# A decoder layer's merge: the first step's eight gate projections placed between the chunks of the second mixer

## The reference, cut to what matters

```python
u = rms_norm(h, mix_norm)
z = u @ w_in + b_in
aq, ak, av, bq, bk, bv, ga, gb = jnp.split(z, np.cumsum(SPLITS)[:-1].tolist(), axis=-1)
ya = dilated_attention(heads(aq), heads(ak), heads(av), rel_bias)
yb = sliding_window_sink_attention(heads(bq), heads(bk), heads(bv), sinks, rel_bias)
merged = jax.nn.sigmoid(ga) * (ya @ w_branch_a) + jax.nn.sigmoid(gb) * (yb @ w_branch_b)
h = h + merged @ w_out
```

## Time and profile before

| | before |
|---|---|
| median of 3 runs | 2120.92 us (2117.65 to 2121.31) |
| profiled execution | 2117.81 us, of it 2116.0 us span |
| PE busy | 2046.4 us, 97% of the span |
| DVE, ACT, POOL busy | 1401.3, 795.7, 177.8 us |
| mean granted clock of PE | 0.986 |

### The profile page before, as it was taken

The page is one execution under the profiler, slowest core; times in us unless marked ns, Lnnn a source line. Parts: engine busy times, 40 slices in busy tenths (PEclk is TensorE's granted clock), DMA queues, the critical chain, the costliest instruction groups (busy, mean ns, idle before and its releaser), DMA issues.

```text
span 2116.0 us, 26479 instructions
## 1 busy us (share of the span) xinstructions
PE 2046.4 (97%) x9404; PEld 1659.8 (78%) x9404; DVE 1401.3 (66%) x2333; ACT 795.7 (38%) x1485; POOL 177.8 (8%) x152
## 2 busy tenths in 40 slices
PE   7999999999999999999879999998999999999996
PEld 5878888888888777777658888887878888888885
DVE  4976667666987454566883444447877666666976
ACT  6343333334454333534452212124342333334453
POOL 4000000000032000241520000003000000000012
PEclk9999999999999999999889999999999999999998
DMA  4232233266444111000002111113222333267433
GB/s 174 80 104 97 103 110 110 75 225 244 138 151 168 40 41 40 31 31 31 21 11 110 50 60 50 50 69 126 75 101 99 105 110 110 75 222 244 139 103 110
DMA packets 82076, 213.21 MB, mean 101 GB/s; under 512 B 8923, under 2 KB 8959, under 8 KB 80032
## 3 DMA queue, kind: packets, MB, share of 16 engines
q1 hardware_dynamic: 69568, 164.66, 22.8%
q10 hardware_dynamic: 11392, 44.06, 5.8%
q0 software_dynamic: 992, 2.88, 0.4%
HBM read 158.58 MB, written 52.98 MB: 100 GB/s over the span
## 4 chain that ended last, share of the span: by engine, by line
PE 88%; DVE 8%; issue 2%; ACT 1%; DMA 0%; POOL 0%; DVEq 0%; SPq 0%; ACTq 0%; POOLq 0%
PE bank L1830 19%; PE bank L1831 19%; PE bank L1832 19%; PE bank L1786 9%; PE bank L1788 8%; PE bank L1787 8%; PE bank L1981 1%; PE bank L2018 1%; PE bank L1994 1%; DVE sp L1669 1%; DVE sp L1625 1%; DVE B_l L1239 1%; DVE wl L1204 1%; DVE op_l L1274 0%; PE bank L2050 0%
## 5 line engine op out<-in xcount | busy, mean ns | idle before, releaser
L1830 PE MATMUL bank<-B_h,op_h 128*128 128x512 f32 x624 | 250.0, 401 | 18.7 <-DVE op_l L1274 13.3
L1786 PE MATMUL bank<-xh,wh 128*128 128x512 f32 x640 | 256.0, 400 | 0.0
L1788 PE MATMUL bank<-xh,wl 128*128 128x512 f32 x640 | 250.0, 391 | 0.0
L1787 PE MATMUL bank<-xl,wh 128*128 128x512 f32 x640 | 249.9, 391 | 0.0
L1830 PE MATMUL bank<-T_h,op_h 128*128 128x512 f32 x640 | 249.1, 389 | 0.2 <-DVE U L1365 0.2
L1832 PE MATMUL bank<-T_h,op_l 128*128 128x512 f32 x640 | 249.0, 389 | 0.0
L1831 PE MATMUL bank<-T_l,op_h 128*128 128x512 f32 x640 | 249.0, 389 | 0.0
L1831 PE MATMUL bank<-B_l,op_h 128*128 128x512 f32 x624 | 246.9, 396 | 0.0
L1832 PE MATMUL bank<-B_h,op_l 128*128 128x512 f32 x624 | 246.5, 395 | 0.0
L1830 PE MATMUL bank<-gs_h,op_h 128*128 128x512 f32 x616 | 240.5, 390 | 0.7 <-DVE gs_l L1308 0.7
L1832 PE MATMUL bank<-gs_h,op_l 128*128 128x512 f32 x616 | 239.7, 389 | 0.0
(11 more groups left out here) (191 smaller groups left out, 3503.5 us busy)
## 6 DMA issues: line engine op xcount, KB each, us to landing
gr<-g_ops SPq DMA_DIRECT2D x154, 256.0 KB, 2.7
raw<-stream SPq DMA_DIRECT2D x56, 512.0 KB, 3.5
gate<-ffn_in SPq DMA_DIRECT2D x44, 512.0 KB, 4.0
up<-ffn_in SPq DMA_DIRECT2D x44, 512.0 KB, 4.9
g_ops<-tT SPq DMA_DIRECT2D x78, 256.0 KB, 2.0
g_ops<-gb SPq DMA_DIRECT2D x58, 256.0 KB, 5.1
A<-ffn_down ACTq DMA_DIRECT2D x6, 1536.0 KB, 8.1
h_spill<-h ACTq DMA_DIRECT2D x32, 256.0 KB, 2.2
```

What stands on the lines that cost most here:

```text
L1786: nc.tensor.matmul(out, wh[slot][:, cols], hi, start=first, stop=False)
L1787: nc.tensor.matmul(out, wh[slot][:, cols], lo, start=False, stop=False)
L1788: return nc.tensor.matmul(out, wl[slot][:, cols], hi, start=False, stop=last)
L1830: nc.tensor.matmul(out, op_h[slot][:, cols], hi, start=first, stop=False, skip_group_check=True)
```

## The change

The four gate tiles of merge step 0 (two tiles of output, two gates each; eight jobs) become jobs of the plan. The list of tiles is now ..., q7, g0, q8, g1, q9, g2, g3, and a job stands in every chunk from 24 to 35, one in chunk 38 and one after chunk 39. For a gate's job DVE writes its product with `rstd` to `stage` (one buffer for each half) instead of `scaled`, and ACT, in place of the bias, issues a DMA of 256 KB to a new HBM buffer `gz`. After its mixing work, POOL issues the loads back to `z_in`, two of 256 KB for each t: t = 0 at once, t = 1 once the transposes of chunk 38 are done (it loads over `sp2`), t = 2 after the last `pv` and the sum of t = 0 (it loads over that t's buffer), t = 3 after the sum of t = 1. Merge step 0 then makes only the 6 and 12 matmuls for each t; ACT takes the sigmoid in place in `z_in` with the gate's bias, and DVE multiplies `z_in` by the bank. The weight units keep their number (56); those of the first step now pass through the plan's slots.

```diff
@@ proj_tiles @@
-    return out + [("q", u) for u in range(A_UNITS + 1, HEAD_UNITS)]
+    for u in range(A_UNITS + 1, HEAD_UNITS):
+        out += [("q", u), ("g", u - A_UNITS - 1)]
+    return out + [("g", GATES - 1)]
@@ attention_plan @@
-            n_jobs = (1, 2, 1, 2)[s] if u < A_UNITS else (0, 1, 0, 1)[s] if u < HEAD_UNITS - 1 else 0
+            n_jobs = (1, 2, 1, 2)[s] if u < A_UNITS else 1 if u < HEAD_UNITS - 1 else (0, 0, 1, 0)[s] if u < HEAD_UNITS else (1, 0, 0, 0)[s]
@@ buffers @@
+    stage = [place(f"stage{s}", [P, HALF], at(20 + 2 * s)) for s in range(2)]
+    z_in = [[place(f"z_in{t}{g}", [P, HALF], at(k)) for g, k in enumerate(ks)] for t, ks in enumerate(((112, 196), (140, 142), (112, 114), (140, 142)))]
@@ gpsimd, behind the mixing @@
+            for t in range(4):
+                pool.wait_ge(gz_out[t], 32)
+                if t == 1:
+                    pool.wait_ge(t_done, 2 * (CHUNKS - 2) + 2)
+                elif t == 2:
+                    pool.wait_ge(pv_out, CHUNKS)
+                    pool.wait_ge(mul_done, 5)
+                elif t == 3:
+                    pool.wait_ge(mul_done, 10)
+                for g in range(2):
+                    pool.dma_start(z_in[t][g][:], gz[t, g]).then_inc(gz_in[t], 16)
@@ scalar, a job of the plan @@
+                    if role == "g":
+                        t = u // 2 * 2 + hf
+                        act.wait_ge(job_scaled, e[1] + 1)
+                        act.dma_start(gz[t, u % 2], stage[hf][:]).then_inc(gz_out[t], 16)
+                        continue
@@ scalar, merge step 0 @@
+                    if first_step:
+                        for gate in range(2):
+                            n = proj_tiles().index(("g", 2 * tile + gate))
+                            act.wait_ge(gz_in[t], 32)
+                            nc.scalar.activation(z_in[t][gate][:], z_in[t][gate][:], ACT.Sigmoid,
+                                                 bias=bias_in[:, n:n + 1]).then_inc(sig_done, 1)
+                        act.wait_ge(mul_done, 5 * job + 5)
+                        nc.scalar.activation(gh[:, tile, hf * HALF:(hf + 1) * HALF], tmp[2][:], ACT.Copy).then_inc(m_high, 1)
+                        if hf:
+                            split_high(unit + MERGE_UNITS + tile, tile, tile, (part_done, 4 * job + 4))
+                        continue
@@ vector, a job of the plan @@
-                    nc.vector.tensor_tensor(scaled[e[1] % 2][:], bank[e[1] % 2][:], rstd[:, hf * HALF:(hf + 1) * HALF],
+                    nc.vector.tensor_tensor(to[:], bank[e[1] % 2][:], rstd[:, hf * HALF:(hf + 1) * HALF],
                                             ALU.mult).then_inc(job_scaled, 1)
@@ vector, merge step 0 @@
+                            dve.wait_ge(sig_done, 2 * job + gate + 1)
+                            dve.wait_ge(part_done, 4 * job + 2 * gate + 2)
+                            nc.vector.tensor_tensor(z[:], z[:], bank[2 * gate + 1][:], ALU.mult).then_inc(mul_done, 2)
@@ tensor, merge step @@
-                    for part in range(4):
+                    for part in (1, 3) if first_step else range(4):
```

More of the change, by code:

```diff
@@ L155, in proj_tiles, with gate_columns, tile_columns @@
         out += [("q", u), ("k", u), ("v", u)]
-    return out + [("q", u) for u in range(A_UNITS + 1, HEAD_UNITS)]
+    for u in range(A_UNITS + 1, HEAD_UNITS):
+        out += [("q", u), ("g", u - A_UNITS - 1)]
+    return out + [("g", GATES - 1)]
+def gate_columns(tile, gate):
+    first = D_IN - 2 * D_MODEL + gate * D_MODEL + tile * P
+    return np.arange(first, first + P)
+def tile_columns(role, u):
+    return gate_columns(u // 2, u % 2) if role == "g" else head_columns(role, u)
 def head_columns(role, u):
@@ L191, in distance_onehot, with outs_to @@
     return out
-JOBS = [(n, hf) for hf in range(2) for n in range(2)] + [(n, hf) for n in range(2, PROJ) for hf in range(2)]
+JOBS = [(n, hf) for hf in range(2) for n in range(2)] + [(n, hf) for n in range(2, TILES) for hf in range(2)]
 JOB_INDEX = {job: j for j, job in enumerate(JOBS)}
+def outs_to(j):
+    tiles = proj_tiles()
+    return sum(tiles[n][0] != "g" for n, _ in JOBS[:j])
 def attention_plan():
     plan = []
-    jobs = iter(range(2 * PROJ))
+    jobs = iter(range(2 * TILES))
     used = []
@@ L490, in build @@
         job_out = sem("job_out")
+        gz_out = [sem(f"gz_out{t}") for t in range(4)]
+        gz_in = [sem(f"gz_in{t}") for t in range(4)]
         qk_done = sem("qk_done")
@@ L1159, in merge_step @@
                 unit = MERGE_0 + MERGE_UNITS * i
-                nc.scalar.activation(gate_bias[:], bias_in[:, bass.ds(PROJ + 4 * i, 4)], ACT.Copy).then_inc(gate_bias_set, 1)
-                act.wait_ge(gate_bias_set, i + 1)
+                first_step = isinstance(i, int) and i == 0
+                if not first_step:
+                    nc.scalar.activation(gate_bias[:], bias_in[:, bass.ds(PROJ + 4 * i, 4)], ACT.Copy).then_inc(gate_bias_set, 1)
+                    act.wait_ge(gate_bias_set, i)
                 for t in range(4):
@@ L1734, in merge_step @@
                         dve.wait_ge(m_low, job)
+                    if isinstance(i, int) and i == 0:
+                        for gate in range(2):
+                            z = z_in[t][gate]
+                            dve.wait_ge(sig_done, 2 * job + gate + 1)
+                            dve.wait_ge(part_done, 4 * job + 2 * gate + 2)
+                            nc.vector.tensor_tensor(z[:], z[:], bank[2 * gate + 1][:], ALU.mult).then_inc(mul_done, 2)
+                        dve.wait_ge(mul_done, 5 * job + 4)
+                        nc.vector.tensor_tensor(tmp[2][:], z_in[t][0][:], z_in[t][1][:], ALU.add).then_inc(mul_done, 1)
+                        dve.wait_ge(m_high, job + 1)
+                        nc.vector.tensor_tensor(gl[:, tile, cols], tmp[2][:], gh[:, tile, cols], ALU.subtract).then_inc(m_low, 1)
+                        if hf:
+                            split_low(unit + MERGE_UNITS + tile, tile, tile)
+                        continue
                     for gate in range(2):
                         dve.wait_ge(part_done, 4 * job + 2 * gate + 1)
-                        if not (isinstance(job, int) and job == 0):
-                            dve.wait_ge(mul_done, 5 * job)
+                        dve.wait_ge(mul_done, 5 * job)
                         nc.vector.tensor_tensor(tmp[gate][:], bank[2 * gate][:], rstd[:, cols], ALU.mult).then_inc(mul_done, 1)
@@ L2126 @@
     b = np.asarray(b_in[0])
-    order = [head_columns(role, u) for role, u in proj_tiles()]
+    order = [tile_columns(role, u) for role, u in proj_tiles()]
     for cols in order:
         columns(w, cols)
-    gates = D_IN - 2 * D_MODEL
     wa, wo = np.asarray(w_branch_a[0]), np.asarray(w_out[0])
@@ L2134 @@
         for t in (2 * i, 2 * i + 1):
-            pair = [np.arange(gates + g * D_MODEL + t * P, gates + g * D_MODEL + (t + 1) * P) for g in range(2)]
+            pair = [gate_columns(t, g) for g in range(2)] if i else []
             order += pair
```

48 lines of the change are left out of this document (31 added, 17 removed).

## The result

| | before | changed |
|---|---|---|
| median of 4 runs each | 2120.38 us (2117.65 to 2121.31) | 2100.47 us (2097.99 to 2103.37) |
| ratio, 95% interval | | 0.991 (0.9895 to 0.9924) |
| profiled execution, of it span | 2117.81, 2116.0 us | 2098.08, 2096.3 us |

The change saves 20 us, 0.9%. The page of the changed kernel, beside the earlier trace rows: PE's share of the chain that ended last has hardly moved (88% before), since almost all of the kernel is PE either way.

The account below looks back on a forecast made before the run. PE bounds the kernel, with 35.3 us idle or slow in the second mixer. Less 4.0, 2.4, 2.0, 2.8 and 2.3 us kept, 21.8 us are gained: 2117.81 becomes 2096.0 us, range 2086 to 2107.

Parts of the forecast that it names:

- the likeliest case: Whole kernel: faster by more than 0.2%, about 4.2 us; chance 0.95.
- the first output product: Sign: from the last projection before chunk 24 to this product, 167 us instead of 188.7.
- the sigmoids of t = 2: Merge step 0: the prediction is wrong if they start later than T+14, T being the start of its first product.
- The ceiling and what stays of it: Second mixer: 35.3 us PE could use, 24.56 idle plus 10.7 slow; waits of 4.0, 2.4 and 2.0 us kept.
- VectorE in the four chunks: Mixer, chunks where POOL mixes: DVE's work 36.0 us, fitting with 3 us to spare in about 39.3 us.
- DVE becomes the bound: Rival, second mixer: DVE keeps its 5.0 us idle, four chunks take 41.0 us instead of 39.3; 2100 us; chance 0.12.
- The slow spells: Second mixer: three of four slow-clock spells go, the one after chunks 35 to 37 stays, 2.8 us.
- the rival's form (on projections): Rival, second mixer: four slow spells stay and fall on projections, 13.6 us instead of 2.8; 2107 us; chance 0.12.
- no spell stays once no wait is over 2.02 us: Second mixer: skill reading "no long gap, no throttling", 2.8 us lower; not used in the sum.
- Merge step 0: Merge's first part: output products start at T+18.6, 2.3 us over PE's 16.3, with t = 2's loads 0.6 us late.
- The gate loads queue behind h: Rival, merge step 0: t = 2's loads move only after h has landed, 6.6 us more; 2103 us; chance 0.12.
- The fetch of h: Merge step 0: lands at about T+14 to T+16, wanted at T+22, so it costs nothing.

Follow-up runs that it names:

- Kernel 4: Against the changed kernel: the eight gate jobs stand behind the last chunk, the queries' jobs where they were before; 2128.17 us.
- kernel 10: Against the changed kernel: DVE makes the `rstd` multiplication of each of the last 14 jobs twice; 2108.09 us.
- kernel 3: Against the changed kernel: the fetch of h is split in two halves, the second issued behind the last sigmoids of the step; 2097.17 us.
- kernel 1: The changed kernel again, unedited; 2101.1 us, 0.9916 beside the kernel before.
- kernel 2: Against the changed kernel: the loads of t = 2 get their own buffer and are issued before the last `pv`, ahead of the fetch of h; 2097.29 us.
- kernel 5: Against the changed kernel: the job of chunks 27 and 31 stands between the product with v and the third `lse` group; 2102.29 us.
- kernel 6: Against the changed kernel: the last two projections stand in chunks 36 and 37 instead of in 38 and behind 39; 2101.95 us.

## Why the prediction was right, and which term was mis-sized

Predicted 2096.0 us, in a range of 2086 to 2107; measured 2100.47, faster, as the likeliest case had it. Against the profiled execution (2098.08) the sum is 2.1 us short; the rest is that execution's distance from its median, which the prediction had allowed for. Part of this closeness is luck: over the mixer and the merge's first part the sum is 3.1 us short (166.9 against 169.97), and 1.0 us came back from stretches that the change doesn't touch. Two of the signs that it named did come out against it: the first output product stands at 169.97 us and not at 167, and the sigmoids of t = 2 start at T+15.1, later than the T+14 at which it called itself wrong. Both are the one term below.

- **The ceiling and what stays of it: right.** The sum gave a mixer of about 148 us; measured 147.3. PE idle was to fall to 8.5 us; it fell to 147.34 - 138.58 = 8.8. The waits stand where they were forecast: 2.02 twice before `lse`; 0.39, 0.60 and 1.40 in chunks 36 and 37; 1.03 and 1.11 at the end. Kernel 4, with the idle time back to the tenth, shows that this filling is the whole gain.
- **VectorE in the four chunks: right.** 36.0 us busy forecast, 35.78 measured (the window lies some 7 us later in the step than that of the earlier trace rows; at the same place, 1014.33 to 1054.99, it is 35.58); the chunks take 40.66 us against 39.3, and the slow spell at 1022 is the difference. The rival "DVE becomes the bound" is not what the trace shows, but kernel 10 says how near it was: one more multiplication a chunk costs 7 us.
- **The slow spells: right in size; the place differs from one execution to the next.** One was kept, behind chunk 37, for 2.8 us. In the profiled execution there was none there; there were two short ones behind the `lse` groups, on the projections of chunks 28 and 32, of 1.5 us each. They are the rival's form (on projections) at the forecast's price. But the trace of kernel 3, whose mixer has the same instructions, has the forecast one, behind the same wait of 1.40 us:

```profile
1106.03 1.97 PE L2074 MATMUL bank<-ident,sp 128*128 128x128 f32 x8 [1.40 <-DVE sp L1735]
1107.93 1.72 PE L2098 MATMUL bank<-pt,v 128*64 128x256 f32 x12
```

It has none on the projection of chunk 28. So what the rows bear out is a cost of some 3 to 4.5 us, and not a place: the mixer takes 147.3 us in the changed kernel and in kernel 1, and 148.8 in kernel 3. By the Trainium skill ("TensorE: Matmul & The Clock Gate", Part 1: The HAM clock gate), activity releases the lower level; the trace agrees in that four spells of 6.8 us shrank to two short ones as the gaps filled, and does not agree with the reading that no spell stays once no wait is over 2.02 us.
- **Merge step 0: the term that was mis-sized.** I took 18.6 us, 2.3 over PE's products; it took 22.6. The chain was as described: loads issued 6.5 us behind the first product (5.8 forecast), wanted at 11.85 (11.8). The step that failed is "with the median of 5.7 [...] 0.6 late": they landed in 8.0 us and were 3.2 late. PE waited 4.06 us instead of 1.2 to 1.8, and the matmuls behind it ran at the lower level, another 1.7 us (5.80 from 1147.69 to 1153.49 for 18 matmuls that take 4.1). Kernels 2 and 3 each take the lateness away and get 18.0 and 18.3 us, the forecast's number. The forecast took the loads' time from loads with nothing large beside them, and the form of the rival "The gate loads queue behind h" (0.12) is what happened: the pair moves when the fetch is through. The rival had its price wrong, since it let the pair take 5.7 us more from there; it takes some 1 us, and the whole term costs 4 us where the rival had 6.6. By the Trainium skill ("DMA: Bandwidth & Descriptors", Anatomy of one DMA — SWDGE (gpsimd) path) the estimate for such a load was 2.6 us; the shortest measured is 2.9 to 3.0, and beside the fetch of h the figure is of no use.
- **The fetch of h: hidden, as said.** No wait for it shows.

The best versions that ran are kernels 2 and 3, both at 2097.2 to 2097.3 us.

## What to carry to other kernels

Where an in-order TensorE idles because every other chunk is thin, independent matmuls made there and carried over through HBM cost less than half of their time: eight projections of 5.44 us made the mixer 18.7 us longer instead of 43.5. Count the lower clock level that follows each gap to the ceiling; here it was a third of it. The price is paid where the results come back: ask which large transfer is in flight when they are loaded, and don't take a small load's time from its own size: here such loads landed about 1 us behind the large one, which was issued 5.4 to 6.6 us before them. Issue small loads that something waits for ahead of it, or split it.

## What the runs showed of the hardware that was not expected

**A small load behind a large one.** 256 KB loads on POOL's queue, issued 5.4 to 6.6 us behind a fetch of 4 MB on ACT's, landed in 6.6 to 9.0 us, 0.8 to 1.7 us behind the fetch; at most 4.6 us when that fetch was halved or the loads were issued ahead of it. In the 5 us from 1138 us the changed kernel's POOL queue moved 0.08 MB beside 2.10 MB on ACT's.

**Slow spells differ between executions of the same instructions.** The first mixer has the same instructions in both kernels. PE's timeline of the kernel before, behind a wait of 1.46 us:

```profile
880.30 2.00 PE L2050 MATMUL bank<-ident,wide 128*128 128x64 f32 x16 [1.46 <-DVE mix L1717]
882.11 0.48 PE L1786 MATMUL bank<-xh,wh 128*128 128x512 f32 x1
882.43 0.39 PE L1787 MATMUL bank<-xl,wh 128*128 128x512 f32 x1
```

and of the changed kernel at the same place:

```profile
879.90 2.15 PE L2125 MATMUL bank<-ident,wide 128*128 128x64 f32 x16 [1.46 <-DVE mix L1780]
881.80 0.77 PE L1861 MATMUL bank<-xh,wh 128*128 128x512 f32 x1
882.37 0.63 PE L1862 MATMUL bank<-xl,wh 128*128 128x512 f32 x1
```

The same wait, and once the matmuls behind it start 0.32 and then 0.23 us apart, once 0.57 and then 0.43. From 709.4 us to the start of the second mixer this makes 272.95 us in the kernel before, 274.12 in the changed one and 275.39 in its repetition, and from the output products to the end 944.99 against 942.81. In the second mixer, too, kernel 1 (the changed kernel again) has one long spell from the third `lse` group of chunk 27 on (3.29 us instead of 2.00, behind the same 2.0 us of wait) and none in chunk 32, where the changed kernel has its second one. A difference of 1 to 3 us between two profiled executions of a 2.1 ms kernel is within this; the comparison of kernels 5 and 6 with 1 rests on their waits more than on their times.
